# A table of places for the raw weight tiles, w_ada in single pieces, M5 ahead of M3 and the first sum two entries ahead, in a fused two-block transformer kernel

## What is computed

```python
x = x + mixed @ w_o
x = x + xo @ w_xo
x = x + (silu(hf @ w_gate) * (hf @ w_up)) @ w_down
x = rmsnorm(x, norm_f_g)
mod = silu(c) @ w_ada + b_ada
shift, scale, gate = split(mod, 3)
h = rmsnorm(x, pre_g) * (1 + scale) + shift
merged = g_a * (y_a @ w_br_attn) + g_p * (y_p @ w_br_pool)
out = x + gate * rmsnorm(merged @ w_out, post_g)
```

## Time and profile before

| | |
|---|---|
| median of 3 runs | 2174.02 us (2172.28 to 2177.65) |
| the profiled execution, its own time | 2175.93 us |
| its span from first to last instruction | 2174.1 us |
| mean granted clock of TensorE | 0.993 |
| TensorE busy | 2085.0 us, 96% |
| VectorE busy | 1681.1 us, 77% |
| ScalarE busy | 1173.4 us, 54% |
| loads | 453.75 MB, 209 GB/s in the mean |

### The profile page before, as it was taken

How to read it: one execution, slowest core, us unless ns; L and a number is a source line. 1 busy time by engine, 2 the same in 40 slices (tenths; PEclk the granted TensorE clock), 3 DMA queues, 4 the chain that set the end, 5 groups by cost and what they waited for, 6 DMA issues and landing times.

```text
span 2174.1 us, 25372 instructions
## 1 busy us (share of the span) xinstructions
PE 2085.0 (96%) x9334; PEld 1700.7 (78%) x9334; DVE 1681.1 (77%) x1839; ACT 1173.4 (54%) x1519; POOL 74.2 (3%) x94
## 2 busy tenths in 40 slices
PE   9999999899999999999999999999899999899998
PEld 7887877778887777787787877877677787778786
DVE  6777777777765778898898888887687767888875
ACT  6655556755554565555455554555655554554453
POOL 1000000000000000000000000000400000000000
PEclk9999999999999999999999999999999999999999
DMA  9444546465444447676567766675455556669753
GB/s 332 155 155 169 174 159 228 167 227 208 155 155 155 155 155 276 240 281 254 213 222 269 278 217 237 233 254 197 135 182 175 174 184 218 227 242 348 232 203 107
DMA packets 218955, 453.75 MB, mean 209 GB/s; under 512 B 14400, under 2 KB 16592, under 8 KB 218704
## 3 DMA queue, kind: packets, MB, share of 16 engines
q1 hardware_dynamic: 212928, 432.07, 56.5%
q0 software_dynamic: 5616, 19.94, 2.8%
q10 hardware_dynamic: 288, 0.13, 0.0%
HBM read 447.88 MB, written 4.19 MB: 208 GB/s over the span
## 4 chain that ended last, share of the span: by engine, by line
PE 57%; DVE 19%; issue 11%; DMA 8%; ACT 5%; POOL 0%; DVEq 0%; ACTq 0%; SPq 0%; POOLq 0%
PE ps L1023 17%; PE ps L1025 17%; PE ps L1024 17%; DVE wlo L2241 8%; DVE raw L2257 3%; DMA raw<-in_w_down_dram 3%; DMA raw<-in_w_up_dram 2%; ACT whi L1535 2%; PE ps L615 1%; DMA raw<-in_w_merge_dram 1%; DMA raw<-in_w_o_dram 1%; DVE FR L1907 1%; DVE FR L1643 1%; DMA raw<-in_w_gate_dram 1%; PE ps L746 1%
## 5 line engine op out<-in xcount | busy, mean ns | idle before, releaser
L2241 DVE TENSOR_TENSOR wlo<-raw,whi 128x1024 fp32r<-128x1024 f32 x832 | 1005.4, 1221 | 307.0 <-ACT whi L1535 300.7
L1535 ACT ACTIVATE whi<-raw 128x1024 fp32r<-128x1024 f32 x840 | 879.9, 1056 | 622.1 <-PE ps L1025 363.1
L1023 PE MATMUL ps<-whi,ah 128*128 128x512 f32 x1618 | 646.5, 400 | 20.2 <-ACT side L1130 12.4
L1025 PE MATMUL ps<-whi,al 128*128 128x512 f32 x1618 | 632.8, 391 | 0.0
L1024 PE MATMUL ps<-wlo,ah 128*128 128x512 f32 x1618 | 631.8, 390 | 0.0
L1023 PEld LDWEIGHTS ps<-whi,ah 128*128 128x128 f32 x1618 | 304.9, 188 | 91.2 <-ACT side L1130 16.2
L1025 PEld LDWEIGHTS ps<-whi,al 128*128 128x128 f32 x1618 | 304.8, 188 | 65.3
L1023 PE MATMUL ps<-whi,bh 128*128 128x512 f32 x862 | 343.4, 398 | 12.0 <-ACT side L1130 9.9
L1024 PEld LDWEIGHTS ps<-wlo,ah 128*128 128x128 f32 x1618 | 305.3, 189 | 61.2 <-issue 0.2
L1025 PE MATMUL ps<-whi,bl 128*128 128x512 f32 x862 | 337.6, 392 | 0.0
L1024 PE MATMUL ps<-wlo,bh 128*128 128x512 f32 x862 | 337.4, 391 | 0.0
(11 more groups left out here) (235 smaller groups left out, 1355.3 us busy)
## 6 DMA issues: line engine op xcount, KB each, us to landing
raw<-in_w_in_dram SPq DMA_DIRECT2D x168, 512.0 KB, 5.7
raw<-in_w_ada_dram SPq DMA_DIRECT2D x96, 512.0 KB, 8.0
raw<-in_w_gate_dram SPq DMA_DIRECT2D x88, 512.0 KB, 7.4
raw<-in_w_up_dram SPq DMA_DIRECT2D x88, 512.0 KB, 6.0
raw<-in_w_down_dram SPq DMA_DIRECT2D x88, 512.0 KB, 7.0
raw<-in_w_merge_dram SPq DMA_DIRECT2D x64, 512.0 KB, 8.0
raw<-in_w_o_dram SPq DMA_DIRECT2D x32, 512.0 KB, 7.1
raw<-in_w_xk_dram SPq DMA_DIRECT2D x32, 512.0 KB, 6.5
```

The source lines that it names most:

```text
L1023: e.matmul(o, xh[:, k, tokens], wh, start=first, stop=False, skip_group_check=more)
L1025: ins = e.matmul(o, xl[:, k, tokens], wh, start=False, skip_group_check=more, stop=kk == 1 and (st.end or st.form in READ))
L1535: done(e.activation(whi[:, n % HALVES, :], raw[:, item % RAWS, :], ACT.Copy), "hi")
L2241: done(e.tensor_tensor(wlo[:, n % HALVES, :], src, whi[:, n % HALVES, :].bitcast(F32), ALU.subtract), "lo")
```

## The change

- `Stream._loads` (new) sorts all items by their first use and gives each the place whose holder is used for the last time earliest. SyncE loads in that order; every engine asks the table (`place`, `loaded`) where item i lies and for what count to wait.
- w_ada is queued one tile at a time ahead of single entries: ahead of the first four halves of u, the first five of d, all six of m, and both halves of the second chunk of ba and bp. There are 96 tiles as before.
- M5 goes ahead of M3. The sum for M5 stands ahead of the low part two entries before M5 (the last but one of the previous pair), and M6's sum behind M3's low part.
- ScalarE takes snapshot s5 in M3's step, directly behind its copy there. `aside` goes on only at steps with jobs, so not at M5, M3 and M1. Sigmoids of the gates rg, ga and gp are in a new list `soon` that goes on at every step, as are VectorE's gate products of a pair's second panel.

```diff
+    def _add_ada(self, todo):
+        if todo:
+            self.ada_before[len(self.entries)] = [len(self.items)]
+            self.items.append(("ada", *todo.pop(0)))
...
+        product("M5", b12, b11, start=True, job=False)
         product("M3", b22, start=True, job=False)
-        product("M5", b12, b11, start=True, job=False)
...
+        todo = {"u": self._early, "d": self._early, "m": self._late}.get(self.panels[s].kind, [])
+        for i, (c, hf) in enumerate((c, hf) for c in range(1, chunks) for hf in range(2)):
+            if i < {"d": 5, "m": 6}.get(self.panels[s].kind, 4):
+                self._add_ada(todo)
+            normal(s, c, hf)
         self.pairs.append(((f, s), at))
+        for form, n in (("M5", at["M5"] - 2), ("M6", at["M3"] + 1), ("M7", at["M1"] + 2),
+                        ("M4", max(at["M2"], at["M6"]) + 1)):
+            self.sums_before[n] = at[form]
...
+        self.loads = sorted(range(len(self.items)), key=lambda i: first[i])
+        self.place, self.nth_load, self.before = {}, {}, {}
+        holds, loaded = [None] * RAWS, [0] * RAWS
+        for item in self.loads:
+            at = min(range(RAWS), key=lambda r: (-1, 0) if holds[r] is None else last[holds[r]])
+            assert holds[at] is None or last[holds[at]] < first[item]
...
             for i, st in enumerate(stream.steps):
-                if st.snap and st.snap[0] != "v":
+                if st.snap and st.snap[0] in ("s1", "s3"):
                     snapshot(*st.snap)
                 make(st.made)
-                aside.step()
+                if st.form == "M3":
+                    snapshot("s5", role[st.p][1])
+                soon.step()
                 if st.job:
+                    aside.step()
                     jobs.step()
...
-                if i >= RAWS:
-                    wait_taken(i - RAWS)
-                if kind == "w":
+                if stream.before[i] is not None:
+                    wait_taken(stream.before[i])
...
-            for i in range(8, len(stream.items)):
+            for i in stream.loads[8:]:
                 load(i)
```

More of the change, by code:

```diff
@@ L376, in _places, with _loads, used @@
         self.free = {what: last[before[what]] if what in before else 0 for what in last}
+    def _loads(self):
+        first, last = {}, {}
+        def used(item, when):
+            first[item] = min(first.get(item, when), when)
+            last[item] = max(last.get(item, when), when)
+        for n, entry in enumerate(self.entries):
+            used(entry.item, (n, 2))
+            for item in self.ada_before.get(n, ()):
+                used(item, (n, 0))
+            if n in self.sums_before:
+                added = self.entries[self.sums_before[n]]
+                for item in (added.item, added.add):
+                    used(item, (n, 1))
+        self.loads = sorted(range(len(self.items)), key=lambda i: first[i])
[4 more added lines that the diff above has]
+            assert holds[at] is None or last[holds[at]] < first[item]
+            loaded[at] += 1
+            self.place[item], self.nth_load[item], self.before[item] = at, loaded[at], holds[at]
+            holds[at] = item
     def lo_count(self, n):
@@ L430, in build_program, with place, loaded @@
         panels, index, role = stream.panels, stream.index, stream.role
+        def place(item):
+            return raw[:, stream.place[item], :]
+        def loaded(item):
+            return s[f"raw{stream.place[item]}"], 16 * stream.nth_load[item]
         def bank_of(p, t):
@@ L1447, in begin @@
                 elif kind == "rg":
-                    aside.start(sigmoids(p, GR, SG, "x"))
+                    soon.start(sigmoids(p, GR, SG, "x"))
                     jobs.start(ret_pair(i))
@@ L2250, in sum_weights @@
                 assert nth == count["t_sum"] + 1
-                for loaded in (item, add):
-                    e.wait_ge(s[f"raw{loaded % RAWS}"], 16 * (loaded // RAWS + 1))
+                for one in (item, add):
+                    e.wait_ge(*loaded(one))
                 if count["lo"]:
@@ L2314, in low_parts @@
                     made[0] += 1
-                    src = raw[:, stream.entries[n].item % RAWS, :]
+                    src = place(stream.entries[n].item)
                     e.wait_ge(s["hi"], n + 1)
@@ L2448, in sync_program @@
                 e.dma_start(XT[j], xT_v[:, 4 * j:4 * j + 4, :]).then_inc(s[f"xt{j}"], 16)
-                load(2 * j)
-                load(2 * j + 1)
-            for i in range(8, len(stream.items)):
+                for i in stream.loads[2 * j:2 * j + 2]:
+                    load(i)
+            for i in stream.loads[8:]:
                 load(i)
```

75 lines of the change are left out of this document (28 added, 47 removed).

## The result

The changed kernel takes 2137.97 us (median of 4, 2134.92 to 2139.39) against 2173.97: the ratio is 0.983, 95% interval 0.9813 to 0.9848. The forecast was 2130, range 2118 to 2156. The medians lie 36.0 us apart. The profiled execution takes 2136.82 us, 39.1 less than that of before; the sum had 45.4.

What follows compares the result with a forecast made beforehand. TensorE, busy 96% of the span, was taken as the bound, with its waits on low parts and snapshots to be won. Terms 23+19+6.4-3 = 45.4 us off the profiled 2175.93 gave 2130.5, stated as 2130, range 2118 to 2156.

Steps and rivals of the forecast that it cites:

- (a): Pair starts in feed-forward and merge: swap, earlier sum and single ada tiles remove TensorE's waits on low parts, 23 us.
- (b): Snapshot s5, mainly pairs 0 to 14 and merge: earlier M5 and deferred work remove TensorE's snapshot waits, 19 us.
- (c): Half-clock stretches of 3.4 us: four of seven follow snapshot waits that go, saving 6.4 us.
- (d): Table of places: saves no instruction, worth counted in (a); SyncE's two long waits a pair go, DMA's idle stretch fills.
- the 14 tiles' 2.3 us deficit: Merge pair's end: loading 14 tiles takes 18.6 us against TensorE's 16.3, covered by tiles let in earlier.
- (e): Squares, scalings, merge sigmoids moved to next normal half: TensorE's turns may wait for scalings, costing 3 us (0 to 8).
- slower rival: In the 19 pairs with ada tiles the early sum blocks VectorE, 3.0 us a pair: 2183 us; chance 0.05.
- Against it: the places are free earlier: Argument against the early sum blocking VectorE: by the table, 8.2 us lie between place free and sum, landing takes 7 to 8.

Runs made afterwards that it cites:

- table_only: Kernel before with only the new table of places and loads in order of first use: gives 24.6 us against 2174.90 us of before.
- aside_all: Changed kernel with aside work going on at every step again, snapshot s5 staying in M3's step: 2143.34 us.
- swap_undone: Changed kernel with M3 ahead of M5 again and snapshot s5 at the next normal half's start; deferral, table, single tiles, early sum stay: 2135.03 us.
- best: Changed kernel with M5's sum not early in pairs 0 and 31, and POOL's loads of mem's second half ahead of root r2: 2127.97 us.
- ring: Changed kernel with the table undone: loads in order of item creation, item i in place i modulo 8, sum still early: 2248.33 us.
- sum_at_m5: Changed kernel with M5's sum directly ahead of M5's own low part in all 40 pairs: 2135.52 us.
- best_no_swap: Changed kernel without the swap, M5's sum not early in pairs 0 and 31, POOL's mem loads ahead of root r2: 2126.99 us.
- deferral_only: Kernel before with only the work on ended panels put off, loads by ring: gives 16.7 us against 2174.90 us of before.

## Why the prediction was right, and where it was not

The waits that the prediction wanted gone went, and the size was a little high: 39.1 us in the profiled execution against 45.4. Of the causes it named for them, two carry the gain (the table and the deferral) and three do not (the swap, the early sum, the single tiles). That the total is near is in part luck: the term of the clock alone was 8.0 us too high, and the other errors cancel to within 2 us.

**(a) Low parts: size right, cause misread.** 13.0 and 6.3 us became 1.0 and 0: 18.3 us in 20 waits, with 0.27 a wait 23.7; the term was 23. But I gave it to the swap, the early sum and the single w_ada tiles, with the table's worth "in (a)". The runs show the table: alone it takes the waits on low parts from 24.3 to 9.5 us, and undoing swap, early sum or single tiles one at a time costs nothing that the medians can tell. What swap, sums and single tiles together are worth there is M5's wait in six pairs of table_only, 3.2 us, or 4.8 with 0.27 a wait.

**(b) Snapshots: right, for half the reasons.** Rows 3's 15.5 us became 4.5 and the merge's 5.8 became 0: with 0.27 a wait 12.4 and 6.6, where the sum had 11.9 and 6.6. The 3.1 us of the earlier trace rows stayed at 3.1, as forecast. The argument counted both the earlier M5 and the deferral; aside_all and swap_undone show that the deferral carries it.

**(c) The clock: this term failed.** It forecast 6.4 us from four stretches at half clock. The changed kernel's profiled execution has eight of 3.4 us ahead of its end, that of before seven: at 1.6 us each the term is -1.6. Four went with their waits, as said, and five came: two in tq1, and one each in pair 7, pair 12 and kv. Two things were wrong in it. Three of the five stand at waits that the sum did not have, 3.94 us in tq1 and 4.74 in pair 7. And one execution's stretches were taken for a property of their waits: the one in kv and the second of pair 12 stand behind waits that before had too (2.61 us in place of 2.62, and 2.67 of 2.29). Pairs 36 and 37 of before show it in hindsight: their waits were no less in sum than pair 38's (4.3, 3.9 and 3.8 us), and they kept full clock.

**(d) The table: right** that DMA would keep up. Merge pairs take 42.2 us with w_ada tiles, so the 14 tiles' 2.3 us deficit was covered. The 358 GB/s of the Trainium skill ("DMA: Bandwidth & Descriptors", Specifications) have no part in this kernel: its 4.2 us a merge pair did not come, and four stretches of 8 us between 8 and 48 us move 374 to 389 GB/s.

**(e) What is moved later: under-sized and misplaced.** I took 3 us for turns that wait for scalings. No turn did. What waited was POOL: the prediction named ScalarE's and TensorE's readers of the deferred work, but did not follow the last squares to VectorE's mean, from there to POOL's root, and to the load queued behind the root. Price in pair 7: a new wait of 4.74 us, or 5.0 with the 0.27, of which one moved line gives back 2.9 (best).

**A term that was missing** is the early sum where nothing is ahead of it. The slower rival described it as a thing of the 19 pairs with w_ada tiles. There the table prevents it (ring shows what it would have been: 2248 us, not the rival's 2183). It happened at one place that I had not looked at, tq1, where the DMA engines are full: 2.5 of the 4.5 us by sum_at_m5, and most of the rest is the stretch at half clock that best_no_swap shows. "Against it: the places are free earlier" holds only once the loads have a lead. In kv, where POOL stands beside it, the early sum costs another 1.3 us (swap_undone against best_no_swap).

Of the merge I had written 42 to 43 us, of waits on snapshots "near 6" (7.6), on low parts "near 4": 11.1, of which 4.7 are pair 7's mem load, 2.4 stand elsewhere in pair 7, 1.6 in pair 31, 1.3 in tq0 and 1.0 in the feed-forward.

## What to carry to other kernels

When tiles live for very different spans, give each load a place by its last use: a ring makes all loads wait behind the longest-lived tile, and the idle DMA shows up much later as a compute engine being late. Moving work of one engine out of the way of a short, awaited copy is worth as much as the copy's whole wait, but follow every result of the moved work through all queues, the DMA issues of another engine's program among them. A consumer moved earlier should be checked at the start of the program first, where loads have no lead.

## What the runs showed of the hardware that was not expected

**VectorE and POOL side by side.** The sum of kv, two entries early, meets POOL's low part:

```profile
1544.74 2.56 POOL L2345 TENSOR_TENSOR wlo<-raw,whi 128x1024 fp32r<-128x1024 f32 x1 [0.24 <-ACT whi L1568]
1544.97 3.41 DVE L2289 TENSOR_TENSOR raw<-raw 128x1024 f32<-128x1024 f32 x1
```

The sum takes 3.41 us in place of 1.23: it is 2.2 us longer, and POOL's instruction runs for 2.3 us more when it starts. The Trainium skill ("GPSIMD Engine Reference", Key points) says that POOL shares its interfaces to the on-chip memory with VectorE, with contention for VectorE instructions that have two inputs there; the trace agrees, and the sum has two. Behind the long sum comes VectorE's scaling (L2043), behind that ScalarE's next copy after 3.75 us idle, and then TensorE stands 1.32. The profile names no releaser for these two waits, so the path is read from the order in time. Of the early sum's 1.3 us in kv, how much is the contention and how much the sum's own 1.2 us no run tells, since the late sum meets no low part of POOL.

**Half clock differs between executions of one kernel.** Seven executions of the kernel before in one comparison had mean granted clocks of 0.990 to 0.995. The two at 0.990 took 2179.05 and 2180.50 us, the two fastest (0.994 and 0.995) 2171.30 and 2170.91. deferral_only was at 0.999 and 2152.56 us in its profiled execution and at 0.994 and 2160.45 in another. So some 8 us of one and the same program come and go with the mean clock. The profiled execution of deferral_only shows that it is not the waits: it has no stretch at half clock ahead of its end, though waits of before that are followed by one are there unchanged. The wait of 2.0 us on VectorE in pair 2 (L680) is one. In before half clock follows it (171.40, 10 matmuls, in the earlier trace rows); in deferral_only, in as long a stretch:

```profile
170.20:173.60 3.40, 3.40 (x17) 2.88 (x18) 3.40 (x4) 1.45 (x2) 0.00 (x0) 1.00 0.57 179
```

A difference of a few us between two kernels should be read only after the stretches at half clock in both have been counted.
